# First two units of the mixers' output projection as one block with two seven-product sets, and the parkings of the side projection moved

## What is computed

```python
h = h + jnp.concatenate([oa, ob, oc, od], axis=-1) @ w_out[i]
y = _rms(h, norm_ffn_g[i])
h = h + (jax.nn.silu(y @ w_gate[i]) * (y @ w_up[i])) @ w_down[i]
y = _rms(h, norm_ple_g[i])
h = h + jax.nn.sigmoid(y @ w_ple_gate[i]) * (p[i] @ w_ple_proj[i])
```

## Time and profile before

| | us |
|---|---|
| median of 3 runs | 1376.66 (1376.61 to 1378.14) |
| the profiled execution, its own time | 1376.73 |
| its span, first to last instruction | 1375.0 |
| TensorE busy | 1369.3 |
| VectorE busy | 1156.1 |
| ScalarE busy | 885.2 |
| GpSimd busy | 151.3 |

### The profile page before, as it was taken

One profiled execution on the slowest core, in us unless ns is written; L12 is line 12 of the kernel. 1 busy time (PEld: TensorE's weight loads), 2 busy tenths in 40 slices (PEclk: granted clock), 3 DMA queues, 4 the chain that ended last, 5 costly groups with the idle time before them and its releaser, 6 DMA issues.

```text
span 1375.0 us, 16935 instructions
## 1 busy us (share of the span) xinstructions
PE 1369.3 (100%) x6169; PEld 1122.6 (82%) x6169; DVE 1156.1 (84%) x1332; ACT 885.2 (64%) x1181; POOL 151.3 (11%) x129
## 2 busy tenths in 40 slices
PE   9999999999999999999999999999999999999998
PEld 7888888888888888888888888888888887777887
DVE  5589986687999988899999889988766769886898
ACT  7476755576777555777756576756666656665554
POOL 2000010011111000111100011100000144430000
PEclk9999999999999999999999999999999999999999
DMA  9776648887999788999987889998987878889686
GB/s 329 252 212 216 201 158 283 278 242 241 296 279 261 234 257 253 271 269 265 281 262 251 254 253 244 284 290 241 310 312 270 278 242 260 257 265 281 210 251 174
DMA packets 183146, 352.93 MB, mean 257 GB/s; under 512 B 13105, under 2 KB 37933, under 8 KB 182936
## 3 DMA queue, kind: packets, MB, share of 16 engines
q1 hardware_dynamic: 160408, 291.66, 64.5%
q0 software_dynamic: 9568, 35.02, 13.2%
q10 hardware_dynamic: 13088, 25.18, 6.1%
HBM read 296.19 MB, written 27.31 MB: 235 GB/s over the span
## 4 chain that ended last, share of the span: by engine, by line
PE 99%; DVE 0%; DMA 0%; ACT 0%; issue 0%; SPq 0%
PE acc L2216 14%; PE acc L2397 14%; PE acc L2400 14%; PE acc L2399 14%; PE acc L2217 14%; PE acc L2218 14%; PE sp L2400 2%; PE sp L2399 2%; PE tp L2400 2%; PE tp L2399 2%; PE sp L2397 2%; PE tp L2397 2%; PE acc L2278 1%; PE sp L2517 1%; PE tp L2533 1%; PE tp L2236 0%
## 5 line engine op out<-in xcount | busy, mean ns | idle before, releaser
L979 ACT ACTIVATE w_hi<-w_raw 128x1024 fp32r<-128x1024 f32 x451 | 472.1, 1056 | 294.8 <-PE acc L2218 188.0
L1419 DVE TENSOR_TENSOR w_lo<-w_raw,w_hi 128x1024 fp32r<-128x1024 f32 x429 | 519.1, 1225 | 131.6 <-ACT w_hi L979 128.7
L2216 PE MATMUL acc<-w_lo,hh 128*128 128x512 f32 x480 | 189.0, 394 | 0.0
L2218 PE MATMUL acc<-w_hi,hl 128*128 128x512 f32 x480 | 186.9, 389 | 0.0
L2217 PE MATMUL acc<-w_hi,hh 128*128 128x512 f32 x480 | 186.9, 389 | 0.0
L2397 PE MATMUL acc<-w_lo,yh 128*128 128x512 f32 x452 | 176.0, 389 | 0.0
L2399 PE MATMUL acc<-w_hi,yh 128*128 128x512 f32 x452 | 175.9, 389 | 0.0
L2400 PE MATMUL acc<-w_hi,yl 128*128 128x512 f32 x452 | 175.9, 389 | 0.0
L979 ACT ACTIVATE w_hi<-wide 128x1024 fp32r<-128x1024 f32 x108 | 114.3, 1060 | 69.6 <-DVE wide L1433 30.2
L1419 DVE TENSOR_TENSOR w_lo<-wide,w_hi 128x1024 fp32r<-128x1024 f32 x108 | 131.5, 1222 | 14.9 <-ACT w_hi L979 14.6
L2216 PE MATMUL acc<-w_lo,yh 128*128 128x512 f32 x352 | 137.4, 390 | 0.0
(11 more groups left out here) (333 smaller groups left out, 2227.6 us busy)
## 6 DMA issues: line engine op xcount, KB each, us to landing
w_raw<-in_w_gate SPq DMA_DIRECT2D x88, 512.0 KB, 5.8
w_raw<-in_w_up SPq DMA_DIRECT2D x88, 512.0 KB, 6.2
w_raw<-in_w_down SPq DMA_DIRECT2D x88, 512.0 KB, 6.4
w_raw<-in_w_in SPq DMA_DIRECT2D x64, 512.0 KB, 4.6
wide<-w_raw POOLq DMA_DIRECT2D x54, 512.0 KB, 5.9
w_raw<-in_swa_w_in ACTq DMA_DIRECT2D x48, 512.0 KB, 5.2
w_raw<-in_w_out SPq DMA_DIRECT2D x32, 512.0 KB, 5.8
w_raw<-in_w_ple_gate SPq DMA_DIRECT2D x32, 512.0 KB, 6.6
```

Source lines behind the costliest of these rows:

```text
L979: act.activation(w_hi[:, v % SPL], src, ACT.Copy).then_inc(hi_ready, 1)
L1419: dve.tensor_tensor(w_lo[:, v % SPL], src, w_hi[:, v % SPL].bitcast(F32), ALU.subtract).then_inc(lo_ready, 1)
L2216: pe.matmul(dst, xh[:, f, tk], w_lo[:, v % SPL, k], start=(f == 0), stop=False)
L2218: last = pe.matmul(dst, xl[:, f, tk], w_hi[:, v % SPL, k], start=False, stop=(f == CK * end + CK - 1))
```

## The change

The first two of the four units of the output projection become a block, `MIXED_PAIR`, with a plan of 20 steps: twelve plain steps and two quads (input chunks 0 and 1, both from mixers whose output is ready early). The two other units stay as they were.

Around it these things move. The sums of the activations for the two quads (`whole_first`, `sum_h(0)`, `h_sums_to_high(0)`, `h_sums_to_low(0)`) are new. The plain chunks come in the order 2, 3, 6, 7, 4, 5 of the input. The split of `T_OA` moves from the fourth step to behind the tenth (step 9, where steps count from 0). The four parkings move from behind loads 12, 16, 24 and 28 of the stage to behind load 8 (two of them) and load 10 (the other two), and the fetch of `T_OA` goes behind them. ACT's wait for all four parkings moves from the first step of `PAIR[0]`'s weight sums into this block, ahead of step 6. The residual's first two columns come at the end of the block, so that the transfers of `T_FFN` and `T_FFN + 1` stand behind loads (2, 7) and (3, 5) of the stage in place of (2, 4) and (3, 4). The sums for the feed-forward (`sum_y`) are made in two halves, the second partly within `PAIR[0]`. The numbers of later blocks shift by one, with no change in their work.

```diff
-OUT_FIRST = (0, 1, 2, 3, 6, 7, 4, 5)
...
+MIXED_PLAN = plain(0, 2, 3) + plain(1, 2, 3) + plain(0, 6) + quad("g", 0) + plain(1, 6) + quad("g", 1) + plain(0, 7)
+MIXED_PLAN += plain(1, 7) + quad("u", 0) + quad("t", 0) + quad("s", 0) + quad("u", 1) + plain(0, 4) + quad("t", 1)
+MIXED_PLAN += quad("s", 1) + plain(0, 5) + plain(1, 4, 5)
+MIXED_AT = dict(whole=1, sums=4, sums_high=6, sums_low=6, turned=9, m1=14, mix=18, mixed_gate=19, bank=19,
+                copied={6: [0], 8: [1]}, summed={0: 9, 1: 13})
...
+MIXED_PAIR = Block(OUT_UNIT, MIXED_PLAN, **MIXED_AT)
...
-            for j in range(NG):
+            b = MIXED_PAIR
+            for i, p in enumerate(b.loads):
+                role = int(p[0] == "u" or p[:2] == ("n", 1))
+                load(b.raw + i, wout_v, OUT_ROWS[p[-1]], CW * role)
+                if i == 7:
+                    put(T_OA)
+                    put_proj(0)
+                    put_proj(1)
+                if i == 9:
+                    put_proj(2)
+                    put_proj(3)
+                    fetch(T_OA)
+            for j in range(2, NG):
                 for c in range(8):
-                    load(START[OUT_UNIT + j] + c, wout_v, OUT_ROWS[c if j else OUT_FIRST[c]], CW * j)
-                    if (j, c) == (0, 7):
-                        move(T_OA)
-                    if j >= 2 and c == 4:
+                    load(START[OUT_UNIT + j] + c, wout_v, OUT_ROWS[c], CW * j)
+                    if (j, c) in ((2, 7), (3, 5)):
                         move(T_FFN + j - 2)
-                    if (j, c) in ((1, 3), (1, 7), (2, 7), (3, 3)):
-                        put_proj(((1, 3), (1, 7), (2, 7), (3, 3)).index((j, c)))
...
+            b = MIXED_PAIR
+            for i in range(len(b.plan)):
+                for q in b.at["copied"].get(i, ()):
+                    copy_tops(b, q)
+                split_high(b.v0 + i)
...
+                if i == b.at["turned"]:
+                    turned_high(T_OA, hh[:, 8:12])
+                if i == b.at["sums_high"]:
+                    h_sums_to_high(0)
+                if i == b.at["m1"]:
+                    copy_m1(b)
...
+                if i == b.at["turned"]:
+                    turned_low(T_OA, hl[:, 8:12], hh[:, 8:12])
+                if i == b.at["sums"]:
+                    wait_half(dve, H_CN + 1)
+                    sum_h(0)
+                if i == b.at["sums_low"]:
+                    h_sums_to_low(0)
+                if i == b.at["mix"]:
+                    mix(b)
+                if i == b.at["mixed_gate"]:
+                    add_mixed_gate(b, 0)
+                if i == b.at["bank"]:
+                    add_bank(b, 0, 1)
+
+            for j in range(2, NG):
+                for c in range(8):
+                    split(START[OUT_UNIT + j] + c)
+                    if (j, c) == (2, 0):
+                        wait_left(dve, OUT_UNIT)
+                        turn(T_FFN, columns(0))
+                    if (j, c) == (2, 1):
+                        add_mixed_up(MIXED_PAIR, 1)
+                    if (j, c) == (2, 2):
+                        add_bank(MIXED_PAIR, 1, 2)
+                    if (j, c) in ((2, 5), (3, 3)):
+                        ffn_turned_low(j - 2)
+                    if (j, c) == (3, 3):
+                        add_resid(OUT_UNIT + 2, 2)
+                    if (j, c) in ((2, 5), (3, 4)):
+                        wait_left(dve, OUT_UNIT + j - 1)
+                        turn(T_FFN + j - 1, columns(j - 1))
+                    if (j, c) in ((2, 6), (2, 7), (3, 0), (3, 1)):
+                        sum_y(0, {6: (0,), 7: (1, 2), 0: (3,), 1: (4,)}[c])
+                    if (j, c) == (3, 5):
+                        y_sums_to_low(0)
+                    if j == 3 and c >= 5:
+                        sum_y(1, {5: (0,), 6: (1, 2), 7: (3, 4)}[c])
+
+
...
+            def before_mixed(i, p):
+                if i == 0:
+                    pe.wait_ge(mix_ready, 1)
+                    wait_half_left(pe, H_PO + 1)
+                if p == ("n", 0, 6):
+                    pe.wait_ge(mix_ready, 2)
+                if p == ("g", 0):
+                    wait_half_left(pe, H_CN + 1)
+                    pe.wait_ge(oa_ready, 1)
+                if p == ("u", 0):
+                    pe.wait_ge(h_sums_low, 1)
+                if p == ("n", 0, 4):
+                    pe.wait_ge(turned_lo, T_OA + 1)
+
+            block(MIXED_PAIR, hh, hl, h_sums_hi, h_sums_lo, None, before_mixed)
```

323 lines of the change are left out of this document (159 added, 164 removed).

## The result

| | before | after |
|---|---|---|
| median, us | 1377.34 (17 runs, 1376.58 to 1379.80) | 1379.42 (17 runs, 1378.49 to 1381.30) |
| ratio after / before | | 1.0015, interval 1.0008 to 1.0022 |
| profiled execution: time, span, us | 1376.73, 1375.0 | 1379.42, 1377.7 |
| matmuls | 6169 | 6163 |
| put of `T_OA` to end of the stage, us | 86.97 | 88.96 |

The change makes the kernel slower by about 2 us, or 0.15%. That is less than the 0.2% that I had set as the bound of what can be told, but the interval of the ratio lies wholly above 1. The forecast was 1376.0, the range ended at 1379.2: the result lies 0.2 us above it.

A forecast was written before the change was run, and what follows sets the result against it. TensorE, busy 1369.3 of 1375.0 us, was taken as the bound. Saving 1.36 us, adding 0.5 for the parkings' wait, 0 for quad 0's sums and 0.1 at the block's end gave -0.8: forecast 1376.0 us, range 1375.0 to 1379.2.

The forecast's parts named there:

- Six matmuls less: Two quads in the new block do seven products each in place of eight, saving 1.36 us, all on TensorE's path.
- Place 1: ACT's wait for the four parkings ahead of step 6, delaying TensorE if past 216.4: cost 0.5 us, between 0 and 5.0.
- X: Time at which ACT's wait for the four parkings ends: taken as 216.9 us, with 221.4 as the bound from above.
- parkings dear: Rival, chance 0.17: parkings take 2.0 to 2.8 us each; X = 218.2 to 221.4; TensorE waits 1.8 to 5.0 us.
- The queue behind the parkings: Transfers issued behind the parkings are delayed but without cost; `T_OA` is back about X + 4, ahead of its use.
- Place 2: Weight sums of quad 0, behind an accumulating DMA landing in 4.9 to 7.7 us: cost 0, nothing beyond Place 1.
- Place 3: End of the block, DVE's mixing, additions and splits, then `T_FFN` with 0.7 us to spare: 0.1 us, between 0 and 0.4.

The follow-up runs named there:

- early parkings: Changed kernel with parkings 0 to 2 issued ahead of the put of `T_OA` and the last right behind it: 1375.98 us, ratio 0.9989; again 1376.06, 0.9991.
- two parkings first: Changed kernel with only parkings 0 and 1 moved ahead of the put of `T_OA`: 1376.51 us, ratio 0.9997 to the kernel before.
- sums in place: Changed kernel, but DVE adds the block's weight sums in the weights' slots, without accumulating DMA or ACT's parkings wait: 1383.20 us, ratio 1.0045; with parkings early 1378.84, 1.0010.
- all parkings ahead of the loads: Changed kernel with parkings 2 and 3 moved ahead of the two loads, all four behind the put of `T_OA`: 1382.97 us, ratio 1.0036 to before.

## Why the prediction was wrong

- **Six matmuls less, 1.36 us:** right. 6163 in place of 6169, and with early parkings the stage is 1.39 us shorter, twice.
- **Place 1, the chain:** right. The need at 216.4 and "wait = X - 216.4" give 1.9 us for X = 218.29; seen, from start to start, were 1.90, and 1.43 more for 1.43 more of X. What the formula leaves out is 0.14 us for the slow matmuls just behind the wait. With X ahead of that point, the wait costs nothing.
- **Place 1, the value of X:** this is the step that failed, 216.9 in place of 218.3. I gave all six transfers behind the put 1.54 us each. Four parkings without loads among them do go at that pace: X is 8.84 us behind the put when they stand ahead of the loads. The two loads between them then make 13.25 of it, 2.2 us each; with two parkings first X is at 10.40, which leaves about as much for each load. They are where the rate falls to 227 and 260 GB/s. The earlier trace rows was read at 216 and 221 us, in mid-stream, though I called the first the rate while the queue fills. The rate at the beginning of a burst of loads should have been read at its beginning, at 209 us, where the kernel before shows 270 GB/s. The issue of the loads, 1.28 us each in place of 0.7, goes with it; which of the two causes the other the runs don't tell. The rival "parkings dear" had the landing (218.2 to 221.4) for another reason: the parkings themselves are not dear.
- **The queue behind the parkings "not so that it counts":** wrong. I followed `T_OA`, which was in time, and not the loads behind it. In the changed kernel they cost 0.27 us openly; the runs with sums in place and with all parkings ahead of the loads show that waits of 2.0 and 3.75 us lie there as soon as nothing else is waited for.
- **Place 2, cost 0 or none beyond place 1:** wrong, 1.1 us (0.75 at `t`, 0.32 at step 14). The upper end of the price of an accumulating DMA was 7.7 us; here, beside a full queue, it took 8.8 (8.6 in the second profile). By my own working 8.8 us need X at 215.5 or earlier, 0.9 us ahead of the 216.4 of place 1, so about that much comes on top of place 1.
- **Place 3, 0.1 us:** right in effect; no wait from 237 to 300 us. `T_FFN` was waited for by 0.28 us on ACT, without consequence.
- **Beyond the stage, 0:** 0.7 us, in a place that no step of mine looked at, and whose cause is open.

By the same sum: -1.36 + 2.04 + 0.27 + 1.07 = +2.0 in the stage, +0.7 behind it, 2.7 between the two profiled executions (1379.42 - 1376.73), 2.1 to 2.6 between the medians. The sign was lost on three terms that were too small, by 1.5, 0.3 and 1.1 us, and all three belong to the same burst of transfers. The weight of 0.50 on the forecast's X was too high for a value between bounds that were 6 us apart. The low end of the range, 1375.0, is 0.25 us lower than its own reason gives (1376.66 - 0.05 - 1.36).

The Trainium skill, "DMA: Bandwidth & Descriptors", "Rules for kernel authors", asks for a DMA to be issued early and waited for late. That holds here: the early parkings follow its first half, with the wait where it was, and give back 3.4 us. Its 358 GB/s in "Where 436 GB/s comes from" is passed here too (384 and 391 GB/s in two of the four stretches from 206 to 218 us), but the mean of the four, weighted by their length, is 326 GB/s: the limit that counted in this burst was neither the page's figure nor the peak of the earlier trace rows.

## What to carry to other kernels

When a wait is moved, ask what the queue it waits for will carry in just that time, and follow every transfer behind it, not only the one that is waited for: here two waits lay behind each other, and removing the first alone brought next to nothing. Transfers with nothing to wait for should go out in the queue's idle time, ahead of the burst; the same edit with three parkings issued about 10 us earlier is worth 3.4 us. Judge such a stage by its own length between two fixed events, which repeated to 0.15 us where whole executions spread by 3. Take the loss of TensorE from the starts of its matmuls: the idle time of its weight loads was about 0.26 us longer at each wait.

## What the runs showed of the hardware

- The pace of transfers in one queue was not one number. While put and parkings were written, slices of 1 us showed 365 to 393 GB/s; the beginning of the weight loads behind them 227 to 272 GB/s with DMA shares of 0.86 to 1.03; 391 GB/s came later (changed kernel, and all parkings ahead of the loads).
- A wait of TensorE can cost more than its length. Behind waits of 1.9 to 2.0 us the granted clock stayed at 1.00; with waits of 3.3, 3.75 and 8.9 us it went to 0.50 (1.2 GHz), and the matmuls then stood 0.43 in place of 0.227 us apart, which together with the restart cost a further 1.7 to 2.9 us.
- An accumulating DMA of 512 KB took 4.5 to 10.1 us to land in these kernels, the longest in the burst of this stage (all parkings ahead of the loads).
